# Hybrid RWKV-7 / S5 / expert trunk on one core: the experts' items worked in pairs, 512 moving columns a matmul, a pair's weights in two transfers

## Chip, cores, metric

One core of one Trainium2 chip. The metric is the device time of the one launch in microseconds. A result counts as faster or slower than before by the medians of runs of the two kernels on one chip.

## What is computed

The kernel runs a trunk of two residual layers on 256 tokens of width 1024, all in float32. Layer 0 is an RWKV-7 time mixer and a dense SwiGLU; layer 1 is an S5 state-space mixer and the expert SwiGLU, of which 2 of 8 experts take each token. The change is in the last of these:

```python
def moe_swiglu(x, router, w_gate, w_up, w_down):
    ...
    top_val, top_idx = lax.top_k(logits, TOP_K)
    gates = jax.nn.softmax(top_val, axis=-1)
    ...
    def block_ffn(args):
        tok, gate, e = args
        xb = xt[tok]
        h = jax.nn.silu(xb @ w_gate[e]) * (xb @ w_up[e])
        return (h @ w_down[e]) * gate[:, None].astype(x.dtype)
```

With D = 1024 and D_EXPERT = 3584, one expert's three matrices are 44 MB, the eight together 352 MB.

## The kernel before

The program is written engine by engine (SP issues DMAs, ACT, PE, DVE, POOL), with semaphores between them. The first 640 us are layer 0, the S5 mixer and its gated output; then come the router and the experts, which are all that the change touches, apart from one buffer's place.

**Blocks and items.** A block is 128 token slots of one expert. With these inputs each expert fills one block, so there are 8 blocks; the last ones go through a loop with a count from a register, with the same body. A block is worked in FM = 28 items. Item n stands for 128 of the 3584 hidden columns, and has 1.5 MB of weights: per partition 2048 floats of gate and up (part a) and 1024 floats of down (part b).

**Two-part numbers.** Every weight and activation is split in a high part, rounded to the matmul's float32r by a copy on ACT, and a low part, the rest by a subtraction on DVE. Each product is made of three matmuls: high by high, high by low, low by high.

**One item.**
- SP: `load_a` and `load_b` (L302, L305) bring parts a and b into one of 7 slots, EXA and EXB. Item n's loads wait until DVE has made the low parts of item n-7 (`m_alo`, `m_blo`): the split copies the weights into WHI and WLO, so the slot is free at once.
- ACT: `hi_a` (L554, two halves of 1024) and `hi_b` (L560) write WHI, of which there are 2; `gate` (L581) takes the silu of the gate half out of PSUM; `turned` (L585) rounds the turned hidden block.
- DVE: `lo_a` (L1650, two halves) and `lo_b` (L1656) write WLO; `product` (L1724) multiplies silu and up; `turned` (L1728) makes the low part of the hidden block.
- PE: `gate_up(n)` (L1180) is 24 matmuls with 256 moving columns (gate and up side by side, 8 k-chunks, 3 products each); `turn(n)` (L1189) transposes the 128x128 hidden block; `down(n)` (L1195) is 6 matmuls with 512 moving columns, added up in two PSUM banks over the 28 items.

**Order.** PE runs `gate_up(n)`, `turn(n-1)`, `down(n-2)` (L1246). ACT and DVE prepare item n+2 while PE works on n. The order on each engine is written out by hand in `first_step` and `steps`.

**Between blocks.** Ahead of a block's end PE gathers the next block's tokens by a one-hot matmul (`gather`, L1205, 16 x 2 matmuls in float32); ACT and DVE split them into XGH and XGL (`gathered`), on which the next `gate_up` waits. When the last `down` of a block is done, ACT and DVE scale and split its output (OH at L594, OL at L1738), and PE adds it to the stream by `scatter` (L1221) in two parts, with a DVE addition (L1744) after each.

Of the kernel before, what the change touches and what calls it, by code (L numbers as in the profile page):

```python
# [15 lines left out]
P = 128  # L16
# [14 lines left out]
NRING, NSLOT = 6, 7  # L31
# [5 lines left out]
FM = FE // P  # L37
WIDE, NARROW = 3 * D, 2 * D
# [39 lines left out]
def build(nc, xT, prm_d, con_d, wsq, wffn, wglu, wmoe, lora1_d, lora2_d, s5p_d, s5b_d, s5c_d, rout_d, out_d):  # L78
    with ExitStack() as ctx:
# [108 lines left out]
        SQG = at("SQG", [P, KC, T], F32, r(96))  # L188
# [7 lines left out]
        EXA = [at(f"EXA{n}", [P, NARROW], F32, o) for n, o in enumerate((r(0), r(8), r(16), r(24), r(32), 0, 8))]  # L196
        EXB = [at(f"EXB{n}", [P, D], F32, o) for n, o in enumerate((r(40), r(44), r(48), r(52), r(56), 16, 20))]
# [45 lines left out]
        def expert_in(part, b, n):  # L243
            return S(f"m{part}_in{n % NSLOT}"), (b * (FM // NSLOT) + n // NSLOT + 1) * 16

        def after(b, n):
            return (b, n) if n < FM else (b + 1, n - FM)

# [21 lines left out]
        def _(sp):  # L270
# [31 lines left out]
            def load_a(b, n, ex):  # L302
                sp.dma_start(EXA[n % NSLOT][:, :], wmoe[ex * FM + n][:, 0:NARROW]).then_inc(expert_in("a", b, n)[0], 16)

            def load_b(b, n, ex):  # L305
                sp.dma_start(EXB[n % NSLOT][:, :], wmoe[ex * FM + n][:, NARROW:WIDE]).then_inc(expert_in("b", b, n)[0], 16)

            sp.wait_ge(S("yq_ps"), KC)
            for n in range(5):
                load_a(0, n, 0)  # L310
                load_b(0, n, 0)
            load_a(0, 5, 0)
            sp.wait_ge(S("glu_used"), 2)
            load_b(0, 5, 0)
            load_a(0, 6, 0)
            load_b(0, 6, 0)
            for n in range(NSLOT, FM):
                sp.wait_ge(S("m_alo"), 2 * (n - NSLOT + 1))
                load_a(0, n, 0)
                sp.wait_ge(S("m_blo"), n - NSLOT + 1)  # L320
                load_b(0, n, 0)

            def load_block(b, ex):
                for n in range(FM):
                    sp.wait_ge(S("m_alo"), b * (2 * FM) + 2 * (n - NSLOT + 1))
                    load_a(b, n, ex)
                    sp.wait_ge(S("m_blo"), b * FM + n - NSLOT + 1)
                    load_b(b, n, ex)

# [12 lines left out]
        def _(act):  # L342
# [211 lines left out]
            def hi_a(b, n, h):  # L554
                if h == 0:
                    act.wait_ge(*expert_in("a", b, n))
                cols = slice(h * D, (h + 1) * D)
                act.activation(WHI[:, n % 2, cols], EXA[n % NSLOT][:, cols], ACT.Copy).then_inc(S("m_ahi"), 1)  # L558

            def hi_b(b, n, down_done=True):  # L560
                act.wait_ge(*expert_in("b", b, n))
                if down_done:
                    act.wait_ge(S("m_used"), b * FM + max(n - 1, 0))
                act.activation(WHI[:, n % 2, NARROW:WIDE], EXB[n % NSLOT][:, :], ACT.Copy).then_inc(S("m_bhi"), 1)  # L564
# [16 lines left out]
            def gate(b, n):  # L581
                act.wait_ge(S("m_ps2"), b * FM + n + 1)
                act.activation(MSG[:, n % 2, :], PS[:, n % 2, 0:P], ACT.Silu).then_inc(S("m_silu"), 1)  # L583

            def turned(b, n):  # L585
                act.wait_ge(S("ht_ps"), b * FM + n + 1)
                act.activation(MHH[:, n % 2, :], PS[:, 4, 0:P], ACT.Copy).then_inc(S("m_hh"), 1)

            def first_step(b, before):
                gate(b, 0)  # L590
                hi_a(b, 2, 0)
                if before:
                    act.wait_ge(S("m_used"), b * FM)
                    act.activation(OH[:, :], flat(PS[:, 2:4, :]), ACT.Copy, scale=GSL[:, 0:1]).then_inc(S("o_hi"), 1)  # L594
                hi_a(b, 2, 1)
                hi_b(b, 0, before)

            def steps(b, first, last):
                for n in range(1, FM):
                    gate(b, n)  # L600
                    turned(b, n - 1)
                    if n == FM - 1 and not last:
                        gathered(b + 1)
                    if n == FM - 1:
                        turned(b, n)
                    if n + 2 < FM or not last:
                        hi_a(*after(b, n + 2), 0)
                        hi_a(*after(b, n + 2), 1)
                    hi_b(b, n, not (first and n == 1))
                    if n == 5:  # L610
                        act.wait_ge(S("selt_ps"), b + 1)
                        act.activation(SELT[:, :], PS[:, 7, 0:T], ACT.Copy).then_inc(S("selt"), 1)

            gathered(0)
            first_step(0, False)
            steps(0, True, False)
            for b in range(1, NEXP - 2):
                first_step(b, True)
                steps(b, False, False)
            act.wait_ge(S("meta"), 1)  # L620
            last_block = act.value_load(META[0:1, 0:1], min_val=NEXP - 1, max_val=NEXP + 2)
            with act.Fori(NEXP - 2, last_block) as b:
                first_step(b, True)
                steps(b, False, False)
            first_step(last_block, True)
            steps(last_block, False, True)
            act.wait_ge(S("m_used"), (last_block + 1) * FM)
# [7 lines left out]
        def _(pe):  # L635
# [544 lines left out]
            def gate_up(b, n):  # L1180
                pe.wait_ge(S("m_alo"), b * (2 * FM) + 2 * n + 2)
                for k in range(KC):
                    cols = slice(k * T, (k + 1) * T)
                    for m, (x, w) in enumerate(((XGH, WHI), (XGH, WLO), (XGL, WHI))):
                        mm = pe.matmul(PS[:, n % 2, 0:T], x[:, k, :], w[:, n % 2, cols], start=k == 0 and m == 0,  # L1185
                                       stop=k == KC - 1 and m == 2)
                mm.then_inc(S("m_ps2"), 1)

            def turn(b, n, first=False):  # L1189
                pe.wait_ge(S("m_mul"), b * FM + n + 1)  # L1190
                if not first:
                    pe.wait_ge(S("m_hl"), b * FM + n)
                pe.transpose(PS[:, 4, 0:P], MHF[:, n % 2, :], ident).then_inc(S("ht_ps"), 1)  # L1193

            def down(b, n):  # L1195
                pe.wait_ge(S("m_blo"), b * FM + n + 1)
                pe.wait_ge(S("m_hl"), b * FM + n + 1)
                for c in range(2):
                    cols = slice(NARROW + c * 512, NARROW + (c + 1) * 512)
                    for m, (x, w) in enumerate(((MHH, WHI), (MHH, WLO), (MHL, WHI))):  # L1200
                        mm = pe.matmul(PS[:, 2 + c, :], x[:, n % 2, :], w[:, n % 2, cols], start=n == 0 and m == 0,  # L1201
                                       stop=n % FM == FM - 1 and m == 2, skip_group_check=True)
                mm.then_inc(S("m_used"), 1)
# [703 lines left out]
```

## Time and profile before

| | us |
|---|---|
| runs (3): median, lowest to highest | 1746.8, 1746.27 to 1753.04 |
| profiled execution, own time | 1744.34 |
| its span | 1742.5 |
| PE busy, share of the span | 1645.1, 94% |
| DVE busy | 1291.5, 74% |
| ACT busy | 975.0, 56% |
| bytes read, mean rate | 418.19 MB, 241 GB/s |

The 1.84 us between the span and the execution's own time lie outside what the profile covers. Busy shares are means over stages with different limits, so they say little of the experts' stage alone, which starts at about 650 us; that stage has to be read from the chain of waits and from the timelines of the engines inside one block. A busy time on PE counts a matmul as longer than it holds the engine, since matmuls overlap: what a matmul costs there is the distance from one start to the next.

### The profile page before, as it was taken

What the parts mean: (1) busy time and instruction counts of PE and PEld (TensorE: products, weight loads), DVE (VectorE), ACT (ScalarE), POOL (GpSimd) and SP (SyncE); (2) the same over time, 40 slices, a digit from 0 to 9 for tenths busy, and PEclk for the clock granted to TensorE, in tenths of its full rate; (3) what the DMA queues carried; (4) which work ended last, traced back from release to release, by engine and by line L of the source; (5) the groups of instructions that cost most, each with busy time, mean ns of one, the idle gap of its engine ahead of it and who ended that gap; (6) DMA issues with size and microseconds to landing.
All of it is one profiled execution on the core that took longest, in us unless ns stands there. A gap on an engine that the chain in (4) does not pass through costs nothing.

```text
span 1742.5 us, 35420 instructions
## 1 busy us (share of the span) xinstructions
PE 1645.1 (94%) x14954; PEld 1526.3 (88%) x14954; DVE 1291.5 (74%) x1878; ACT 975.0 (56%) x1476; POOL 83.9 (5%) x69
## 2 busy tenths in 40 slices
PE   6999799899998887999999999999999999999996
PEld 5788787899998767999999999999999999999995
DVE  6355433796866435888988988988988988988985
ACT  1332211577431123776776776776776776776774
POOL 0004300200003500000000000000000000000000
PEclk8999998999996996999999999999999999999998
DMA  7230001554524231998998998998998998998980
GB/s 308 73 121 2 4 4 29 190 191 150 181 86 195 97 159 62 356 355 307 352 361 307 349 363 304 352 362 306 353 357 302 353 363 309 347 361 308 350 324 25
DMA packets 76252, 421.53 MB, mean 242 GB/s; under 512 B 8624, under 2 KB 8880, under 8 KB 41280
## 3 DMA queue, kind: packets, MB, share of 16 engines
q1 hardware_dynamic: 75744, 418.18, 64.8%
q8 instruction: 119, 1.95, 0.4%
q0 software_dynamic: 352, 1.10, 0.2%
q14 instruction: 37, 0.30, 0.1%
HBM read 418.19 MB, written 1.05 MB: 241 GB/s over the span
## 4 chain that ended last, share of the span: by engine, by line
PE 86%; DVE 7%; ACT 2%; POOL 2%; issue 2%; DMA 0%; SPq 0%; DVEq 0%; POOLq 0%; ACTq 0%
PE PS L1185 33%; PE PS L1201 17%; PE PS L1023 11%; PE PS L657 5%; PE PS L1131 2%; DVE WLO L1653 2%; PE PS L1209 2%; PE PS L1008 2%; PE PS L1193 1%; PE PS L803 1%; DVE WLO L1658 1%; PE PS L639 1%; PE PS L820 1%; PE PS L1097 1%; PE PS L672 1%
## 5 line engine op out<-in xcount | busy, mean ns | idle before, releaser
L1653 DVE TENSOR_TENSOR WLO<-EXA,WHI 128x1024 fp32r<-128x1024 f32 x448 | 530.3, 1221 | 88.4 <-ACT WHI L558 87.8
L1185 PE MATMUL PS<-WHI,XGH 128*128 128x256 f32 x1792 | 510.0, 285 | 3.1 <-DVE XGL L1734 2.4
L1185 PE MATMUL PS<-WLO,XGH 128*128 128x256 f32 x1792 | 507.8, 283 | 0.0
L1185 PE MATMUL PS<-WHI,XGL 128*128 128x256 f32 x1792 | 507.7, 283 | 0.0
L558 ACT ACTIVATE WHI<-EXA 128x1024 fp32r<-128x1024 f32 x448 | 450.3, 1060 | 0.0
L1185 PEld LDWEIGHTS PS<-WHI,XGH 128*128 128x128 f32 x1792 | 340.8, 190 | 12.3 <-DVE XGL L1734 2.6
L1185 PEld LDWEIGHTS PS<-WLO,XGH 128*128 128x128 f32 x1792 | 340.6, 190 | 8.1
L1185 PEld LDWEIGHTS PS<-WHI,XGL 128*128 128x128 f32 x1792 | 340.7, 190 | 0.0
L1658 DVE TENSOR_TENSOR WLO<-EXB,WHI 128x1024 fp32r<-128x1024 f32 x224 | 273.0, 1219 | 2.4 <-ACT WHI L564 2.4
L564 ACT ACTIVATE WHI<-EXB 128x1024 fp32r<-128x1024 f32 x224 | 236.2, 1055 | 8.8 <-PE PS L1201 8.8
L583 ACT ACTIVATE MSG<-PS 128x128 f32<-128x128 f32 x224 | 62.1, 277 | 270.2 <-PE PS L1185 270.2
L1201 PE MATMUL PS<-WHI,MHH 128*128 128x512 f32 x448 | 195.3, 436 | 5.2 <-DVE WLO L1658 5.2
L1201 PE MATMUL PS<-WHI,MHL 128*128 128x512 f32 x448 | 176.9, 395 | 0.0
L1201 PE MATMUL PS<-WLO,MHH 128*128 128x512 f32 x448 | 175.4, 392 | 0.0
L1023 PE MATMUL PS<-FH,WHI 128*128 128x256 f32 x352 | 101.7, 289 | 6.1 <-DVE FL L1474 5.8
L1201 PEld LDWEIGHTS PS<-WHI,MHL 128*128 128x128 f32 x448 | 84.3, 188 | 19.8
L1023 PE MATMUL PS<-FL,WHI 128*128 128x256 f32 x352 | 100.5, 285 | 0.0
L1023 PE MATMUL PS<-FH,WLO 128*128 128x256 f32 x352 | 100.3, 285 | 0.0
L1201 PEld LDWEIGHTS PS<-WHI,MHH 128*128 128x128 f32 x448 | 84.3, 188 | 17.4 <-DVE WLO L1658 7.0
L1201 PEld LDWEIGHTS PS<-WLO,MHH 128*128 128x128 f32 x448 | 85.3, 190 | 10.3
L1726 DVE TENSOR_TENSOR MHF<-MSG,PS 128x128 f32<-128x128 f32 x224 | 62.8, 280 | 32.0 <-ACT MSG L583 32.0
L1023 PEld LDWEIGHTS PS<-FH,WHI 128*128 128x128 f32 x352 | 68.3, 194 | 6.9 <-issue 6.4
(370 smaller groups left out, 2398.4 us busy)
## 6 DMA issues: line engine op xcount, KB each, us to landing
EXA<-in_wmoe SPq DMA_DIRECT2D x224, 1024.0 KB, 7.8
EXB<-in_wmoe SPq DMA_DIRECT2D x224, 512.0 KB, 5.6
FRA<-in_wffn SPq DMA_DIRECT2D x22, 1024.0 KB, 5.8
RING<-in_wsq SPq DMA_DIRECT2D x16, 1024.0 KB, 4.9
FRB<-in_wffn SPq DMA_DIRECT2D x22, 512.0 KB, 3.7
GLUW<-in_wglu SPq DMA_DIRECT2D x8, 1024.0 KB, 12.2
LORA<-in_lora SPq DMA_DIRECT2D x1, 1536.0 KB, 22.1
LORA<-in_lora SPq DMA_DIRECT2D x1, 1152.0 KB, 18.9
```

Source lines behind the costliest of these rows:

```text
L558: act.activation(WHI[:, n % 2, cols], EXA[n % NSLOT][:, cols], ACT.Copy).then_inc(S("m_ahi"), 1)
L564: act.activation(WHI[:, n % 2, NARROW:WIDE], EXB[n % NSLOT][:, :], ACT.Copy).then_inc(S("m_bhi"), 1)
L583: act.activation(MSG[:, n % 2, :], PS[:, n % 2, 0:P], ACT.Silu).then_inc(S("m_silu"), 1)
L657: mm = pe.matmul(out, w[:, h * D + k * P:h * D + (k + 1) * P], x[:, k, :], start=k == 0, stop=k == KC - 1)
L1008: mm = pe.matmul(half(W_BANK[t - 12], h), w[:, h * D + k * P:h * D + (k + 1) * P], T1[:, k, :], start=k == 0, stop=k == KC - 1)
L1023: mm = pe.matmul(out, a, b, start=start and k == 0 and n == 0, stop=stop and k == k_count - 1 and n == 2, skip_group_check=True)
L1131: mm = pe.matmul(half(4 + t % 4, h), GLUW[:, t, h * D + k * P:h * D + (k + 1) * P], HN[:, k, :], start=first and h == 0 and k == chunks[0] ...
L1185: mm = pe.matmul(PS[:, n % 2, 0:T], x[:, k, :], w[:, n % 2, cols], start=k == 0 and m == 0, stop=k == KC - 1 and m == 2)
L1201: mm = pe.matmul(PS[:, 2 + c, :], x[:, n % 2, :], w[:, n % 2, cols], start=n == 0 and m == 0, stop=n % FM == FM - 1 and m == 2, skip_group ...
L1653: tt(WLO[:, n % 2, cols], EXA[n % NSLOT][:, cols], WHI[:, n % 2, cols].bitcast(F32), ALU.subtract)\
L1658: tt(WLO[:, n % 2, NARROW:WIDE], EXB[n % NSLOT][:, :], WHI[:, n % 2, NARROW:WIDE].bitcast(F32), ALU.subtract)\
L1726: tt(MHF[:, n % 2, :], MSG[:, n % 2, :], PS[:, n % 2, P:2 * P], ALU.mult).then_inc(S("m_mul"), 1)
```

## The change

Items are worked in pairs, 14 a block (NP). PE, ACT and DVE take a pair where they took an item:

- `gate_up(p)` is 24 matmuls with 512 moving columns, the two items' columns side by side (two runs of 256); one PSUM bank holds a pair. The transposes of the pair before stand in its middle, after 12 matmuls. `down(p)` is 12 matmuls of 512, as two `down` before.
- The high parts lie in WH (4 items). The low part is written over the loaded weights (LOA and LOB have the addresses of EXA and EXB), so WLO is gone and its room holds more of WH.
- A slot is now free only when PE is done with it: the load of part a waits for `m_ps2` (the `gate_up` of the slot's last user), that of part b for `m_used` (its `down`).
- There are 4 slots of two items; PAIR_SLOT gives pair p's slot. Slot 3 is used by pairs 3 and 13 alone, so a slot comes back after 4 pairs for p = 0 to 6 and after 3 pairs for p = 7 to 12.
- A transfer brings two items: 2 MB for part a, 1 MB for part b.
- ACT and DVE take a part a in one instruction of 2048 elements instead of two of 1024, and the silu, product and turned steps of a pair in one of 256 instead of two of 128.
- The first high and low parts of block 0 are no longer interleaved with the norm before the router (`root(3)`, `norm(3)`); SQG, the squares of that norm, lies elsewhere.

```diff
-NRING, NSLOT = 6, 7
+NP = FM // 2
+PAIR_SLOT = (0, 1, 2, 3, 0, 1, 2, 0, 1, 2, 0, 1, 2, 3)
...
+        EXA = [at(f"EXA{n}", [P, 2, NARROW], F32, o) for n, o in enumerate((r(0), r(16), r(32), 0))]
+        EXB = [at(f"EXB{n}", [P, 2, D], F32, o) for n, o in enumerate((r(48), r(100), 16, r(64)))]
+        LOA = [at(f"LOA{n}", [P, 2, NARROW], F32R, o) for n, o in enumerate((r(0), r(16), r(32), 0))]
+        LOB = [at(f"LOB{n}", [P, 2, D], F32R, o) for n, o in enumerate((r(48), r(100), 16, r(64)))]
+        WH = at("WH", [P, 4, WIDE], F32R, 24)
...
+        def slot_before(p):
+            return max(x for x in range(p - NP, p) if PAIR_SLOT[x % NP] == PAIR_SLOT[p])
...
+            def load_a(b, p, ex):
+                two = wmoe[bass.ds(ex * FM + 2 * p, 2)].rearrange("e p c -> p e c")
+                sp.dma_start(EXA[PAIR_SLOT[p]][:, :, :], two[:, :, 0:NARROW]).then_inc(expert_in("a", b, 2 * p)[0], 16)
...
+            def load_block(b, ex, first=False):
+                for p in range(NP + 1):
+                    if p < NP:
+                        if not first or slot_before(p) >= 0:
+                            sp.wait_ge(S("m_ps2"), b * NP + slot_before(p) + 1)
+                        elif p == 3:
+                            sp.wait_ge(S("glu_used"), 2)
+                        load_a(b, p, ex)
+                    if p > 0:
+                        if not first or slot_before(p - 1) >= 0:
+                            sp.wait_ge(S("m_used"), b * NP + slot_before(p - 1) + 1)
+                        elif p == 4:
+                            sp.wait_ge(S("xt_ps"), 2)
+                        load_b(b, p - 1, ex)
...
-            hi_a(0, 0, 0)
             root(3)
-            hi_a(0, 0, 1)
-            hi_a(0, 1, 0)
-            hi_a(0, 1, 1)
+            hi_a(0, 0)
+            hi_a(0, 1)
...
+            def step(b, p, first, last):
+                fresh = first and p == 0
+                gate(b, p)
+                if p == NP - 1 and not last:
+                    gathered(b + 1)
+                if p + 2 < NP or not last:
+                    hi_a(*after(b, p + 2)[:1], 2 * after(b, p + 2)[1])
+                if p == 0 and not first:
                     act.wait_ge(S("m_used"), b * NP)
                     act.activation(OH[:, :], flat(PS[:, 2:4, :]), ACT.Copy, scale=GSL[:, 0:1]).then_inc(S("o_hi"), 1)
+                if p + 2 < NP or not last:
+                    hi_a(after(b, p + 2)[0], 2 * after(b, p + 2)[1] + 1)
+                turned(b, p)
+                if p + 1 < NP or not last:
+                    if not fresh:
+                        act.wait_ge(S("m_used"), b * NP + p)
+                    for e in range(2):
+                        hi_b(after(b, p + 1)[0], 2 * after(b, p + 1)[1] + e)
...
+            def gate_up(b, p, turn_of=None):
+                pe.wait_ge(S("m_alo"), b * FM + 2 * p + 2)
                 for k in range(KC):
+                    if k == KC // 2 and turn_of:
+                        turn(*turn_of)
                     cols = slice(k * T, (k + 1) * T)
+                    hi, lo = WH[:, 2 * (p % 2):2 * (p % 2) + 2, cols], LOA[PAIR_SLOT[p]][:, :, cols]
+                    for m, (x, w) in enumerate(((XGH, hi), (XGH, lo), (XGL, hi))):
+                        mm = pe.matmul(PS[:, p % 2, :], x[:, k, :], w, start=k == 0 and m == 0, stop=k == KC - 1 and m == 2)
...
+            def block(b, first, last):
                 pe.wait_ge(S("xg_lo"), b + 1)
+                for p in range(NP):
+                    if p > 0:
+                        gate_up(b, p, (b, p - 1))
+                        if p == 1 and not first:
+                            scatter(b, 0)
+                        down(b, p - 1)
+                        if p == 1 and not first:
+                            scatter(b, 1)
+                    elif first:
+                        gate_up(b, 0)
+                    else:
+                        gate_up(b, 0, (b, -1))
+                        down(b, -1)
...
```

DVE's step follows the same order as ACT's: product, `lo_a` of item 2p+4, `lo_a` of item 2p+5, `turned`, `lo_b` of the two items of pair p+1; with `gathered` after the product in the last step, OL between the two `lo_a` in step 0, and the two additions (L1744) around the first `lo_a` in step 1.

**SP, the end of a block.** The built order of the transfer queue before, three slots on either side of block 0's end (all transfers wait for DVE's low parts; EXA is part a, EXB part b, the digit is the slot):

```order
L303 DMA EXA4_152<-in_wmoe 128x2048 [waits m_alo]
L306 DMA EXB4_159<-in_wmoe 128x1024 [waits m_blo]
L303 DMA EXA5_153<-in_wmoe 128x2048 [waits m_alo]
L306 DMA EXB5_160<-in_wmoe 128x1024 [waits m_blo]
L303 DMA EXA6_154<-in_wmoe 128x2048 [waits m_alo]
L306 DMA EXB6_161<-in_wmoe 128x1024 [waits m_blo]
```

and of the change, from pair 11 of block 0 to pair 1 of block 1:

```order
L314 DMA EXA1_149<-in_wmoe 128x2x2048 [waits m_ps2]
L318 DMA EXB0_152<-in_wmoe 128x2x1024 [waits m_used]
L314 DMA EXA2_150<-in_wmoe 128x2x2048 [waits m_ps2]
L318 DMA EXB1_153<-in_wmoe 128x2x1024 [waits m_used]
L314 DMA EXA3_151<-in_wmoe 128x2x2048 [waits m_ps2]
L318 DMA EXB2_154<-in_wmoe 128x2x1024 [waits m_used]
L318 DMA EXB3_155<-in_wmoe 128x2x1024 [waits m_used]
L314 DMA EXA0_148<-in_wmoe 128x2x2048 [waits m_ps2]
L314 DMA EXA1_149<-in_wmoe 128x2x2048 [waits m_ps2]
```

Part a of pair 11 is the first row, of pair 12 the third, of pair 13 the fifth (slot 3); the part a of the next block's pair 0 stands behind both last parts b.

**DVE, the first items of block 1.** Before:

```order
L1726 TENSOR_TENSOR MHF<-MSG,PS 128x128
L1653 TENSOR_TENSOR WLO<-EXA_150,WHI 128x1024
L1738 SCALAR_TENSOR_TENSOR OL<-PS,GSL,OH 128x1024
L1653 TENSOR_TENSOR WLO<-EXA_150,WHI 128x1024
L1658 TENSOR_TENSOR WLO<-EXB_155,WHI 128x1024
L1726 TENSOR_TENSOR MHF<-MSG,PS 128x128
L1730 TENSOR_TENSOR MHL<-PS,MHH 128x128
L1653 TENSOR_TENSOR WLO<-EXA_151,WHI 128x1024
L1744 TENSOR_TENSOR HT<-HT,PS 128x1024
```

and now, over the first two pairs:

```order
L1725 TENSOR_TENSOR MHF<-MSG,PS 128x256
L1650 TENSOR_TENSOR LOA_158<-EXA_150,WH 128x2048
L1738 SCALAR_TENSOR_TENSOR OL<-PS,GSL,OH 128x1024
L1650 TENSOR_TENSOR LOA_158<-EXA_150,WH 128x2048
L1730 TENSOR_TENSOR MHL<-PS,MHH 128x256
L1656 TENSOR_TENSOR LOB_161<-EXB_153,WH 128x1024 x2
L1725 TENSOR_TENSOR MHF<-MSG,PS 128x256
L1744 TENSOR_TENSOR HT<-HT,PS 128x1024
L1650 TENSOR_TENSOR LOA_159<-EXA_151,WH 128x2048
L1744 TENSOR_TENSOR HT<-HT,PS 128x1024
```

The output's split and the two additions now fall into two pairs' time where they fell into three items' time.

## Rows read from the trace of the kernel before

**Rows 1.** The page: 40 slices (PE, granted clock, DMA, GB/s)
```profile
PE   6999799899998887999999999999999999999996
PEclk8999998999996996999999999999999999999998
DMA  7230001554524231998998998998998998998980
GB/s 308 73 121 2 4 4 29 190 191 150 181 86 195 97 159 62 356 355 307 352 361 307 349 363 304 352 362 306 353 357 302 353 363 309 347 361 308 350 324 25
```
**Rows 2.** Chain of waits inside a block (start, us, what)
```profile
1248.02 2.88 PE PS L1185 x24
1250.90 0.11 PE PS L1193
1251.01 1.39 PE PS L1201 x6
1252.39 2.88 PE PS L1185 x24
```
**Rows 3.** Chain of waits at a block's end: gathers, a piece of down, scatter, slots
```profile
795.85 0.92 PE PS L1201 x4
796.77 3.57 PE PS L1209 x32
...
809.41 1.06 ACT WHI L558
...
816.91 1.28 DVE OL L1738
...
838.97 0.22 PE PS L1215 x2
839.18 0.34 PE PS L1217 x4
...
927.09 3.57 PE PS L1209 x32
```
**Rows 4.** DVE and ACT inside a block (start, us, engine, line, names)
```profile
1252.36 2.36 DVE L1653 TENSOR_TENSOR WLO<-EXA,WHI 128x1024 fp32r<-128x1024 f32 x2 [0.48 <-ACT WHI L558]
1254.63 1.22 DVE L1658 TENSOR_TENSOR WLO<-EXB,WHI 128x1024 fp32r<-128x1024 f32 x1
1255.31 0.28 ACT L583 ACTIVATE MSG<-PS 128x128 f32<-128x128 f32 x1 [1.09 <-PE PS L1185]
```
**Rows 5.** Groups by line and form: instructions of the sizes the change uses
```profile
L1361 DVE TENSOR_TENSOR KK<-KK,PS 128x2048 f32<-128x2048 f32 x1 | 2.3, 2287 | 5.4 <-PE PS L711 5.4
L1592 DVE TENSOR_TENSOR FHF<-FSG,PS 128x256 f32<-128x256 f32 x22 | 9.2, 419 | 21.2 <-ACT FSG L527 21.2
L612 ACT ACTIVATE SELT<-PS 128x256 fp32r<-128x256 f32 x8 | 3.0, 380 | 0.0
L378 ACT ACTIVATE KSQ<-KK x1: 1902/1902/1902, 77.4 to 77.4; 128x2048 f32<-128x2048 f32 x1
```
**Rows 6.** Block 0's first items, the norm before it, and the last items
```profile
645.48 1.28 ACT L348 ACT_TABLE_LOAD   x1
647.23 1.75 DVE L1292 RECIPROCAL NT<-NT 128x256 f32<-128x256 f32 x1 [0.29 <-ACT NT L348]
678.81 4.61 PE PS L1185 x24
688.20 0.08 DVE OV L1709
...
691.50 0.16 DVE META L1722
692.49 2.67 PE PS L1201 x6
1717.51 0.13 PE PS L1193
1720.20 1.67 PE PS L1201 x6
```
**Rows 7.** Windows: time, busy of five engines, clock, DMA share, GB/s
```profile
600.00:625.00 25.00, 25.00 (x118) 22.00 (x117) 4.54 (x10) 4.74 (x11) 0.00 (x0) 1.00 1.00 413
718.00:796.00 78.00, 78.00 (x557) 73.47 (x556) 69.86 (x90) 58.37 (x90) 0.00 (x0) 1.00 0.97 357
840.00:925.00 85.00, 85.00 (x607) 80.11 (x607) 75.88 (x102) 63.43 (x97) 0.00 (x0) 1.00 0.97 359
```
**Rows 8.** Part a of one item alone (issued at 598.4), and of 718 to 925 us
```profile
DMA to landing us min/median/max: 5.2/5.2/5.2
DMA to landing us min/median/max: 5.5/8.0/9.5
```

More of the change, by code:

```diff
@@ L598, in steps, with gate @@
-            def steps(b, first, last):
[L599 to L612, printed above, removed]
+            def gate(b, p):
+                act.wait_ge(S("m_ps2"), b * NP + p + 1)
+                act.activation(MSG[:, :, :], PS[:, p % 2, :].rearrange("p (e t) -> p e t", e=2)[:, :, 0:P], ACT.Silu)\
+                   .then_inc(S("m_silu"), 1)
@@ L1187, in gate_up, with turn @@
                 mm.then_inc(S("m_ps2"), 1)
[L1189 to L1202, printed above, removed]
+            def turn(b, p):
+                pe.wait_ge(S("m_mul"), b * NP + p + 1)
+                for e in range(2):
+                    tr = pe.transpose(PS[:, 4, e * P:(e + 1) * P], MHF[:, e, :], ident)
+                tr.then_inc(S("ht_ps"), 1)
@@ new lines, in down @@
+            def down(b, p):
+                pe.wait_ge(S("m_blo"), b * FM + 2 * p + 2)
+                pe.wait_ge(S("m_hl"), b * NP + p + 1)
+                for e in range(2):
+                    for c in range(2):
+                        cols = slice(c * 512, (c + 1) * 512)
+                        hi, lo = WH[:, (2 * p + e) % 4, NARROW + c * 512:NARROW + (c + 1) * 512], LOB[PAIR_SLOT[p % NP]][:, e, cols]
+                        for m, (x, w) in enumerate(((MHH, hi), (MHH, lo), (MHL, hi))):
+                            mm = pe.matmul(PS[:, 2 + c, :], x[:, e, :], w, start=p == 0 and e == 0 and m == 0,
+                                           stop=p % NP == NP - 1 and e == 1 and m == 2, skip_group_check=True)
@@ new lines, in step @@
+            def step(b, p, first, last):
+                product(b, p)
+                if p == NP - 1 and not last:
+                    gathered(b + 1)
+                if p == 1 and not first:
+                    add(b, 0)
+                more_a, more_b = p + 2 < NP or not last, p + 1 < NP or not last
+                if more_a:
+                    lo_a(after(b, p + 2)[0], 2 * after(b, p + 2)[1])
+                if p == 0 and not first:
+                    out_low(b)
+                if p == 1 and not first:
+                    add(b, 1)
+                if more_a:
+                    lo_a(after(b, p + 2)[0], 2 * after(b, p + 2)[1] + 1)
+                turned(b, p)
+                if more_b:
+                    for e in range(2):
+                        lo_b(after(b, p + 1)[0], 2 * after(b, p + 1)[1] + e)
+                if p == 3:
+                    dve.wait_ge(S("selt"), b + 1)
+                    dve.tensor_copy(GSL[:, :], PS[:, 7, T:T + 1]).then_inc(S("gsl"), 1)
+                if p == 4 and not last:
+                    dve.wait_ge(S("gsl"), b + 1)
+                    if isinstance(b, int):
+                        one_hot(b + 1)
+                    else:
+                        one_hot(dve.value_load(META[0:1, bass.ds(b + 13, 1)], min_val=0, max_val=2 * NEXP - 1))
@@ L1779, in _ @@
+            def steps(b, first, last):
+                for p in range(NP):
+                    step(b, p, first, last)
+                    if p == 0 and first:
+                        blocks_in_order()
             gathered(0)
-            first_step(0, False)
-            blocks_in_order()
+            lo_b(0, 0)
+            lo_b(0, 1)
             steps(0, True, False)
             for b in range(1, NEXP - 2):
-                first_step(b, True)
                 steps(b, False, False)
```

194 lines of the change are left out of this document (56 added, 138 removed).

## The prediction

> **What bounds the kernel now.** I read the slices first: from the seventeenth on, which is the experts' stage, PE is at 9, the granted clock is at its upper level (2.4 GHz), and the DMA digits repeat 9, 9, 8 with 302 to 363 GB/s [rows 1]. PE and DMA both look full, so the chain of waits has to say which one ends last. Inside a block it is PE alone: 24 matmuls of 256 columns in 2.88 us, a transpose in 0.11, six matmuls of 512 in 1.39, and at once the next item [rows 2]. An item takes 1252.39 - 1248.02 = 4.37 us, a block's 28 take 122.4. DVE is close behind: 2.36 + 1.22 us of low parts an item besides two small steps, with 0.48 us of idle that ends on ACT [rows 4]. DMA moves 1.5 MB an item, 357 to 359 GB/s, at a busy share of 0.97 [rows 7]; but it is paced by PE through the slots, and the same queue moved 413 GB/s at 600 to 625 us, when seven items were queued at once.
>
> From one gather to the next a block takes 927.09 - 796.77 = 130.3 us [rows 3]. Its PE work is 122.4 + 3.57 (gather) + 0.22 + 0.34 (slots) + 16 scatter matmuls of 256 columns at 0.12 = 1.92, in all 128.5. So PE stands for 1.8 us a block, all of it at the block's start, where the chain leaves PE for ACT and DVE [rows 3].
>
> **The change, part by part.** g is the moment at which PE ends `gate_up` of a pair.
>
> 1. *Matmul width.* A matmul of 256 columns costs 2.88 / 24 = 0.120 us [rows 2], one of 512 costs 0.92 / 4 = 0.230 [rows 3]. A pair's gate and up were 48 of the first (5.76) and are now 24 of the second (5.52): 0.24 us less a pair, 8 x 14 = 112 pairs, **-26.9 us**. Bounds: 0 if a moving operand in two runs of 256 costs what two matmuls did (0.240), -26.9 if it runs as that of `down`; no row shows less for 512. I take the second, since the engine, type and width are those of `down`. The Trainium skill (TensorE: Matmul & The Clock Gate, Back-to-back issue gap) gives an isolated gap of N / 2.4 + 2.5 ns. By it two matmuls of 256 would cost only 2.5 ns more than one of 512, 0.06 us a pair, and this term would be -6.7 us. The rows speak against it: 0.120 and 0.230 are 13 and 17 ns above N / 2.4, so joining two saves 10 ns. `down` keeps its 12 matmuls a pair, the two transposes keep 0.11 each.
>
> 2. *DVE and ACT inside a block.* An instruction of 2048 elements takes 2.29 us on DVE and 1.90 on ACT, one of 256 takes 0.42 and 0.38 [rows 5]; 1024 cost 1.22 and 1.06 [rows 4, 3]. A pair: DVE 2 x 2.29 + 2 x 1.22 + 2 x 0.42 = 7.9 us, ACT 2 x 1.90 + 2 x 1.06 + 2 x 0.38 = 6.7, against PE's 5.52 + 2.77 (12 x 0.231) + 0.22 = 8.51. Neither binds by its sum. In order: ACT's silu to g + 0.4, high parts to g + 4.2; PE transposes at g + 2.8 + 2.8 = g + 5.6, ACT's turned to g + 6.1, `hi_b` to g + 8.2. DVE's product to g + 0.9, low parts to g + 6.9, turned to g + 7.3, where `down` wants it at g + 8.5; `lo_b` to g + 9.7, the next product to g + 10.1, and the next low part can't start before g + 8.5 + 2.3 = g + 10.8. So PE has 1.2 us to spare and DVE 0.7. **0 us**. If that cover goes, `down` is late by what the low parts are late.
>
> 3. *Block starts.* XGL is ready at g + 0.4 + 1.0 + 1.2 = g + 2.7, PE wants it after `down` at g + 2.8: hidden by a tenth. In step 0 the output's split waits for the last `down` (g + 2.8): OH to g + 3.9, DVE's OL to 5.8; `scatter` part 0 is due after the next `gate_up` at g + 8.5. Then comes `down` (2.8), and part 1 waits for DVE's addition. The order shows it behind turned, two `lo_b` and a product: DVE is there at about g + 11, the addition ends at 12.3 beside `down`'s g + 12.2. PE stands some 0.3 us where it stood 1.8. Seven starts by 1.5: **-10.5 us** (bounds: 0, if DVE's backlog is carried on as now, and -12.6, all of it).
>
> 4. *Block 0's start.* Before, 678.8 to 796.8 was 118.0 us for 112.8 of work (26 `gate_up` at 2.88, 25 `down` at 1.39, 25 transposes, the slots): 5.2 lost, to the clock at its lower level (24 matmuls in 4.61 instead of 2.88, six in 2.67 [rows 6]) and to DVE's table of blocks (688.2 to 691.7 [rows 6]). Now that table stands behind step 0. By the durations of part 2: the first `gate_up` ends at 686.0, the second at 691.8, DVE's turned at 693.1 (PE waits 1.3); table to 698.8, product to 699.2, where the transposes want it at 698.7 (0.5); low parts and turned to 704.0 against a third `gate_up` at 702.2 (1.8). With the clock's 1.7 that is 5.3, and the stalls may cost clock again. **+0.5 us**, give or take 3.
>
> 5. *The norm before.* DVE's reciprocal came at 647.23 because a high part stood ahead of the square root and its table load [rows 6]. Without it the load can start 1 us earlier: **-0.9 us**. The high and low parts that stood there fit where ACT and DVE wait for PE's transposes and gather.
>
> 6. *The end.* After the last `gate_up` PE had one `down`, a transpose at 1717.51, and the last `down` at 1720.20, held by `lo_b` [rows 6]. Now `lo_b` was made a step earlier, and only the turned step is waited for, about 1.2 us: **-1.8 us**.
>
> 7. *Transfers.* The price no row gives. Slots are free later (after PE, not after DVE), so there are 3 or 4 pairs of lookahead less the time PE takes. Where it is 3 (pairs 7 to 12), part a of pair p+3 is issued at g(p), and ACT wants it at g(p+1) + 0.3 = g + 8.8. If it lands at g + L, the chain is L + 1.9 + 2.3 + 2.3 + 0.4 to `down`(p+1), then 2.8 and 5.5 to g(p+3), which is due at 25.5: PE waits only if L is over 10.2 us. Bounds for L: one item's part a, alone, took 5.2 us [rows 8]; another 1 MB at 413 GB/s is 2.5 more, 7.7. In the steady stretch it took 8.0 in the middle [rows 8], queued behind its predecessor; 1 MB more at 357 GB/s is 2.9, 10.9. The queue should be shorter than that, since part b of 1 MB was issued 5.7 us before, so I take 8.5 to 9: no wait, with 0.5 us a block for those that scatter past 10.2, **+4 us**. By rate: a block's 44 MB in 126 us is 350 GB/s, but SP issues nothing from g(2) + 2.8 to g(4), since pair 7 waits for slot 0's second user. Less 2.8 us for issue and landing, 21 MB must move from g(4) to ACT's use of pair 13 at g(11): 59.9 - 2.8 = 57.1 us, 367 GB/s.
>
> Sum: -26.9 - 10.5 + 0.5 - 0.9 - 1.8 + 4 = -35.6 us. The profiled execution took 1744.3, so 1708.7; it lies 2.5 us below the runs' median of 1746.8, from which the sum gives 1711.2. I say **1710 us**.
>
> **Rivals.**
> - *The transfers' rate takes over.* If the queue, under load from ACT and DVE, can't pass 358 GB/s, the 21 MB take 58.6 + 2.8 = 61.4 us where 59.9 are there: 1.5 us a block instead of 0.5, **1718 us**; at 350 GB/s it is 2.9 a block, 1729. For it: share 0.97 at 357 to 359, and landing at 8.0 us. Against it: 413 in the same queue. The Trainium skill (HBM Reference, Specifications (TRN2)) gives 358 GB/s as the effective rate of one core, and says that a core alone goes well above it. The trace's 413 agrees with the second. Chance 0.18.
> - *512 columns in two runs bring less.* A pair's gate and up at 5.7 us or more: **1730 to 1737 us**. The skill's isolated gap would put it at 1730. For it: the moving operand is no longer one run. Against it: [rows 2, 3]. Chance 0.12.
> - *A late transfer holds ACT: slower than before.* ACT waits for part a ahead of turned, so a late part a holds `down`, and with it the release of the next slots. Over L = 10.2 each pair of 7 to 12 is longer by (L - 10.2) / 3, a block by 2 x (L - 10.2). All of the gain (35.6 + 4 = 39.6, 4.9 a block) is gone at L = 12.7. If a transfer of two items takes as long as two of one item in the steady stretch less one fixed part (5.2 - 2.5 = 2.7, so 16.0 - 2.7 = 13.3 us), a block is 6.2 longer: **1757 us**. For it: no transfer of 2 MB in this trace, the two items' rows lie 1.5 MB apart, and the slots are fewer. Against it: the 8.0 us already hold a queue of one item. Chance 0.07.
> - That the change doesn't do what it says is ruled out by the built order: 24 matmuls of 128x512 a pair, and transfers of 128x2x2048.
>
> **How the numbers follow.** Forecast 0.58 (1701 to 1716; block 0's start and the other starts may each be 3 to 6 us off), the rate 0.18 (to 1729), the columns 0.12 (to 1738), late transfers 0.07 (half of it above 1755), anything else 0.05. About 0.5% (8.7 us) is what a measurement of this kernel can tell from no change. Faster, under 1738: 0.58 + 0.18 + 0.11 = 0.87. Within 0.5%: 0.01 of the columns' case, 0.03 of the late transfers', 0.02 of the rest, 0.06. Slower, over 1755.5: the other 0.04 of the late transfers' and 0.03 of the rest, 0.07. For 8 in 10 the range takes the forecast's, the rate's, and the columns' in part: 1701 to 1732.
>
> **What would show it.** In the profile after: `gate_up`'s 24 matmuls in 5.5 us and a pair every 8.5 us in the chain (5.76 says the columns bring nothing); gather to gather 126 us; PE's idle time at a block's start under 0.5 us; DVE idle ahead of each first low part by about a microsecond, ended by ACT; part a from issue to landing under 10 us, DMA near 370 GB/s in a block's second half and a hole in the first. ACT's first high part released by a DMA in most pairs would make me wrong toward the slower side. PE released by the turned low part inside a block would say that part 2 was cut too fine.

## The result and the profile after

| | before | after |
|---|---|---|
| median of 4 runs, us | 1746.5 | 1699.9 |
| lowest to highest | 1743.1 to 1753.0 | 1698.8 to 1704.5 |
| ratio, 95% interval | | 0.9734 (0.970 to 0.977) |
| span of the profiled execution | 1742.5 | 1697.9 |

The change makes the kernel 46.6 us faster by these medians. 35.6 were forecast, as 1710 us, with a range from 1701: the sign and the mechanism were right, the size wasn't, and the time lies 1 us outside the range. Two repetitions of the pair of kernels (e1 and e9 below) gave 41.7 and 41.9 us, with the change at 1701.6 and 1702.0 us. So the last 5 us of the gain are not firm, and the 1 us outside the range could have fallen either way; what was wrong in the forecast has to be read from the stages.

The slices of the page, against [rows 1]:

```profile
PE   5999789899998996999999999999999999999996
PEclk8999998899997897999999999999999999999998
...
GB/s 309 81 110 16 5 4 27 151 190 170 160 152 199 3 273 1 223 367 410 273 374 417 276 374 411 281 375 411 273 385 410 272 384 402 279 385 401 273 389 27
```

PE is still full. The transfers are less even than they were: a block's three slices read some 275, 375 and 410 GB/s, where they read some 305, 350 and 360. The first is the hole in the issues, where pair 7 waits for its slot; the last is above anything the steady stretches before had.

The chain of waits inside a block (start, us, what), against [rows 2]:

```profile
1219.87 2.72 PE PS L1208 x12
1222.59 2.72 PE PS L1191 x12
1225.31 0.22 PE PS L1197 x2
1225.53 2.75 PE PS L1191 x12
1228.28 2.72 PE PS L1208 x12
```

A pair takes 1228.28 - 1219.87 = 8.41 us. Two items took 8.75, and 8.51 were forecast. Twelve matmuls of 512 columns take 2.72 us, 0.2267 each: `down`'s (L1208) too, which cost 0.230 to 0.231 before. Only the twelve behind the transposes take 0.03 more.

The block's period and its start in the chain of waits, against [rows 3]; L1216 is the gather, L1234 and L1235 are scatter:

```profile
1040.69 3.57 PE PS L1216 x32
...
1165.30 3.57 PE PS L1216 x32
...
1177.29 2.95 PE PS L1191 x12
...
1192.58 2.75 PE PS L1208 x12
1195.33 0.10 issue
1195.43 0.36 PE PS L1234
```

Gather to gather is 124.61 us (130.3 before). 14 x 8.41 + 3.57 + 1.92 + 0.56 is 123.8, so PE loses 0.8 us at a block's start, in three places for the most part: 0.23 in the first `gate_up` (2.95 for 2.72), 0.34 around scatter's second part, and 0.14 in the twelve matmuls behind the slots (2.86 for 2.72 at 1214.04). It was 1.8.

The groups by line, against [rows 4, 5]:

```profile
L1650 DVE TENSOR_TENSOR LOA<-EXA,WH 128x2048 fp32r<-128x2048 f32 x224 | 504.5, 2288 | 87.0 <-ACT WH L563 87.0
L563 ACT ACTIVATE WH<-EXA 128x2048 fp32r<-128x2048 f32 x224 | 416.8, 1910 | 4.3 <-DMA EXA<-in_wmoe 3.9
```

The durations are those taken (2.29 and 1.90). DVE's idle ahead of the first low part of a pair is 87 us over 112 pairs, 0.8 each, and ends on ACT. ACT was held by a transfer 3.9 us in all, and PE never.

Block 0's start in the chain of waits, against [rows 6]; L1708 is the first of the table's instructions on DVE:

```profile
679.89 5.75 PE PS L1191 x24
...
692.71 2.27 DVE LOB L1656 x2
694.98 0.08 DVE OV L1708
...
698.43 0.32 DVE MHF L1725
698.75 4.40 DVE LOA L1650 x2
703.15 0.34 DVE MHL L1730
703.50 0.14 issue
703.63 3.00 PE PS L1208 x12
```

As walked: the table (from 694.98, L1708 on) between the low parts and the product, and `down` of pair 1 at 703.6, held by both.

**Where the 44.6 us of the two profiled executions lie**, from one marker of the chain to the next:

| stage | before | after | difference |
|---|---|---|---|
| start to the S5 output's matmuls | 598.35 | 601.42 | +3.07 |
| to the router's first matmul | 53.98 | 53.04 | -0.94 |
| to block 0's first `gate_up` | 26.48 | 25.43 | -1.05 |
| to the gather of block 1 | 117.96 | 111.61 | -6.35 |
| six blocks, gather to gather | 781.75 | 747.63 | -34.12 |
| last gather to the end | 163.98 | 158.77 | -5.21 |

The first row is code that the change doesn't touch. The later profiles put it anywhere from 593.7 to 604.1 us, so a single execution's span carries some 5 us either way that is nobody's doing, and I compare stages where less than that matters. The third row is chance too: it is block 0's gather, whose 32 matmuls took 6.27 us before and 5.22 after, at a granted clock of 0.56 (670 to 676 us) and 0.72 (672.3 to 677.5). In the later profiles of kernels with the change it took 5.17 to 6.76 us.

### The profile page after: what moved, and what is told of

It is laid out like the page before. It is cut to its first block, busy times and chain, and to the rows that moved or that the text cites. A ratio compares the mean times of both kernels' runs of the same rounds, so it can differ in the third digit from the quotient of the medians.

```text
span 1697.9 us, 28219 instructions
## 1 busy us (share of the span) xinstructions
PE 1607.5 (95%) x12266; PEld 1378.8 (81%) x12266; DVE 1257.5 (74%) x1430; ACT 942.0 (55%) x1028; POOL 83.9 (5%) x69
## 3 DMA queue, kind: packets, MB, share of 16 engines
HBM read 418.19 MB, written 1.05 MB: 247 GB/s over the span
## 4 chain that ended last, share of the span: by engine, by line
PE 91%; DVE 4%; POOL 2%; issue 1%; ACT 1%; DMA 0%; SPq 0%; POOLq 0%; DVEq 0%
PE PS L1191 36%; PE PS L1208 18%; PE PS L1026 11%; PE PS L660 5%; PE PS L1134 2%; PE PS L1011 2%; PE PS L1216 2%; PE PS L1197 1%; PE PS L642 1%; PE PS L806 1%; PE PS L823 1%; PE PS L1100 1%; PE PS L675 1%; PE PS L1234 1%; POOL SPS L1836 1%
## 5 line engine op out<-in xcount | busy, mean ns | idle before, releaser
L1650 DVE TENSOR_TENSOR LOA<-EXA,WH 128x2048 fp32r<-128x2048 f32 x224 | 504.5, 2288 | 87.0 <-ACT WH L563 87.0
L563 ACT ACTIVATE WH<-EXA 128x2048 fp32r<-128x2048 f32 x224 | 416.8, 1910 | 4.3 <-DMA EXA<-in_wmoe 3.9
L1191 PE MATMUL PS<-WH,XGH 128*128 128x512 f32 x896 | 360.8, 403 | 2.4 <-DVE XGL L1734 2.4
L1191 PE MATMUL PS<-WH,XGL 128*128 128x512 f32 x896 | 350.7, 391 | 0.0
L1191 PE MATMUL PS<-LOA,XGH 128*128 128x512 f32 x896 | 350.1, 391 | 0.0
L1656 DVE TENSOR_TENSOR LOB<-EXB,WH 128x1024 fp32r<-128x1024 f32 x224 | 264.2, 1221 | 8.5 <-ACT WH L567 8.5
L567 ACT ACTIVATE WH<-EXB 128x1024 fp32r<-128x1024 f32 x224 | 224.1, 1052 | 0.0
L1191 PEld LDWEIGHTS PS<-WH,XGL 128*128 128x128 f32 x896 | 168.2, 188 | 35.6
L1208 PE MATMUL PS<-WH,MHH 128*128 128x512 f32 x448 | 174.7, 390 | 4.2 <-DVE MHL L1730 4.2
L1208 PE MATMUL PS<-LOB,MHH 128*128 128x512 f32 x448 | 174.5, 389 | 0.0
L1208 PE MATMUL PS<-WH,MHL 128*128 128x512 f32 x448 | 174.4, 389 | 0.0
L1208 PEld LDWEIGHTS PS<-WH,MHH 128*128 128x128 f32 x448 | 84.1, 188 | 22.3 <-issue 5.2
L1208 PEld LDWEIGHTS PS<-WH,MHL 128*128 128x128 f32 x448 | 84.1, 188 | 17.5
L1208 PEld LDWEIGHTS PS<-LOB,MHH 128*128 128x128 f32 x448 | 84.2, 188 | 17.1
```

The costliest lines, as they stand in the source:

```text
L563: act.activation(WH[:, n % 4, 0:NARROW], EXA[PAIR_SLOT[n // 2]][:, n % 2, :], ACT.Copy).then_inc(S("m_ahi"), 1)
L567: act.activation(WH[:, n % 4, NARROW:WIDE], EXB[PAIR_SLOT[n // 2]][:, n % 2, :], ACT.Copy).then_inc(S("m_bhi"), 1)
L1191: mm = pe.matmul(PS[:, p % 2, :], x[:, k, :], w, start=k == 0 and m == 0, stop=k == KC - 1 and m == 2)
L1208: mm = pe.matmul(PS[:, 2 + c, :], x[:, e, :], w, start=p == 0 and e == 0 and m == 0, stop=p % NP == NP - 1 and e == 1 and m == 2, skip_gro ...
L1650: tt(LOA[slot][:, n % 2, :], EXA[slot][:, n % 2, :], WH[:, n % 4, 0:NARROW].bitcast(F32), ALU.subtract)\
L1656: tt(LOB[slot][:, n % 2, :], EXB[slot][:, n % 2, :], WH[:, n % 4, NARROW:WIDE].bitcast(F32), ALU.subtract)\
```

## Experiments

Theory: PE alone ends last inside a block; the gain is what 512 columns save a matmul, and the forecast took too high a price for a matmul of 512. Rivals: the gain comes from working in pairs whatever the width; the transfers' size or the larger instructions on ACT and DVE carry part of it; the transfers limit it.

**e1. The change once more.**

> The changed kernel itself, once more. Its 1699.9 us should come back within 0.3%. What varies from one profiled execution to the next is to be read from it: the experts' stage (gather to gather) at 124.60 us within 0.1 whatever the execution, and the start of the S5 output's matmuls (598.35 us before, 601.42 after, in code the change doesn't touch) anywhere within about 3 us if that shift was chance, at 601.4 again if the change made it.

Measured: 1701.6 us (ratio to before 0.9759, 0.9727 to 0.9791; the unchanged kernel measured 1743.3 here). Gather to gather was 124.60 us, and the S5 output's matmuls began at 597.75. A second repetition, e9, gave 1702.0 us (0.9751, 0.9725 to 0.9776), 124.60 and 593.65. The 3.07 us were chance; the block's period repeats to 0.02 us. Block 0's start doesn't repeat as well: its first 24 matmuls took 7.32 us in e1, at a granted clock of 0.77, and 5.75 in the first profile and in e9, at 1.00.

**e2. The width alone.**

```diff
                     for m, (x, w) in enumerate(((XGH, hi), (XGH, lo), (XGL, hi))):
-                        mm = pe.matmul(PS[:, p % 2, :], x[:, k, :], w, ...)
+                        for e in range(2):
+                            mm = pe.matmul(PS[:, p % 2, e * T:(e + 1) * T], x[:, k, :], w[:, e, :], ...)
```

> Pairs, buffers and transfers kept, but each matmul of 512 moving columns in gate_up made as two of 256 (the weights loaded twice). If the gain lies in the matmuls' width, at 0.120 us for 256 columns and 0.2267 for 512: 24 x 0.0133 = 0.32 us more a pair, a pair at 8.73, gather to gather 129.1, 112 pairs 36 us, 1736 us. If it lies in working in pairs (fewer waits, instructions and PSUM turns) and not in the width: 1700 to 1705 us. By the Trainium skill's isolated gap (TensorE: Matmul & The Clock Gate, Back-to-back issue gap) two of 256 cost 2.5 ns more than one of 512: 1707 us.

Measured: 1726.3 us (0.9886, 0.9861 to 0.9911), 24.7 above e1, whose neighbour in the same job it was; gather to gather 128.33. The chain of waits:

```profile
1252.48 2.87 PE PS L1192 x24
1255.35 0.22 PE PS L1200 x2
1255.57 2.88 PE PS L1192 x24
1258.44 2.75 PE PS L1211 x12
1261.19 2.88 PE PS L1192 x24
```

A pair takes 8.71 us, 0.30 more than in the change, and a block 3.73 more: 30 us over 8 blocks. (14 x 0.30 is 4.2; the rest comes back at a block's start. The stage from gather 0 to the end grew by 29.8; the medians' 24.7 has the chance of the first stages in it.) The expectation had 36 us and a block of 129.1. So the width carries 0.30 of the 0.34 us that a pair gained. The pair costs 0.04 less than two items even at 256 columns, and the timeline shows where: matmul starts in `down`, behind 256-column matmuls (start, duration, engine, line),

```profile
1258.28 0.40 PE L1211 MATMUL PS<-WH,MHH 128*128 128x512 f32 x1
1258.51 0.40 PE L1211 MATMUL PS<-LOB,MHH 128*128 128x512 f32 x1
...
1259.67 0.39 PE L1211 MATMUL PS<-WH,MHH 128*128 128x512 f32 x1
1259.89 0.39 PE L1211 MATMUL PS<-LOB,MHH 128*128 128x512 f32 x1
...
1261.03 0.40 PE L1192 MATMUL PS<-WH,XGH 128*128 128x256 f32 x2
```

The first six stand (1259.67 - 1258.28) / 6 = 0.232 us apart, the other six (1261.03 - 1259.67) / 6 = 0.227. Twice six (the down of two items) are all dear ones; of twelve in a row half are. By the isolated gap of the Trainium skill (TensorE: Matmul & The Clock Gate, Back-to-back issue gap), which the page gives for a single matmul, the width would be worth an estimated 6.7 us, and e2 less 6.7 is 1719.6. The change in the same job measured 1701.6, 18 us below it, so that gap doesn't describe matmuls which each load their weights, as these do.

**e3. One item a transfer.**

```diff
-                sp.dma_start(EXA[PAIR_SLOT[p]][:, :, :], two[:, :, 0:NARROW])...
+                for e in range(2):
+                    sp.dma_start(EXA[PAIR_SLOT[p]][:, e, :], two[:, e, 0:NARROW])...
```

(part b likewise, the waits for 32 instead of 16)

> Each transfer of two items made as two of one item, issued one behind the other behind the same wait. If the transfers are hidden and their size doesn't matter: 1700 us, within 3. If the two-item transfers are what lets the queue reach 410 GB/s: landing goes up from 7.7 us in the second half of a block to over 10, DMA back to under 370 GB/s over a block's last part, and the time by up to 1.6 us a block, 1713 us.

Measured: 1697.6 us (0.9726, 0.9702 to 0.975), gather to gather 124.60. The transfers' size is worth nothing here: they are hidden either way. Nor does the queue need transfers of two items for its rate: in the same part of the same block it moved 383 GB/s (1101 to 1166 us) where e1 moved 383 (1095 to 1160; e3's block begins 6 us later). Part a of one item landed in 7.2 us in the middle.

**e4. The kernel before with the transpose inside gate_up.**

```diff
                 for k in range(KC):
+                    if k == KC // 2 and turn_of:
+                        turn(*turn_of)
...
-                    gate_up(b, n)
-                    turn(b, n - 1)
+                    gate_up(b, n, (b, n - 1))
                     down(b, n - 2)
```

> The kernel before, with the transpose of the item before moved from behind gate_up into its middle, for the items from 3 on. Nothing is removed, so the time should stay at 1746 us, within 4. If a matmul of 512 columns in down took 0.230 us because it stands behind a transpose, down's six now take 0.2267 each (1.36 us), and the 256-column matmuls behind the transpose become a few ns longer. If the 0.230 belongs to down itself (its two banks, its six in a row), they stay at 0.230 and the pair's 0.2267 has another cause.

Measured: 1743.0 us (0.9989, 0.9976 to 1.0003). No transpose stands near `down` now (the timeline, start and duration):

```profile
1253.11 0.40 PE L1203 MATMUL PS<-WHI,MHH 128*128 128x512 f32 x1
1253.34 0.40 PE L1203 MATMUL PS<-WLO,MHH 128*128 128x512 f32 x1
...
1254.27 0.39 PE L1203 MATMUL PS<-WHI,MHL 128*128 128x512 f32 x1
1254.50 0.28 PE L1187 MATMUL PS<-WHI,XGH 128*128 128x256 f32 x1
```

(1254.50 - 1253.11) / 6 = 0.232: still slow. A transpose right ahead isn't needed for it. Nor does the price belong to `down` itself, whose twelve cost 0.2267 each inside a pair of the change. With e2 what is left of the tried causes is a matmul's place behind shorter ones: a matmul of 512 costs 0.232 as one of the first six behind matmuls of 256, and 0.2267 later. The change shows it too: `down` behind the 256-column matmuls of scatter (1192.58 above) takes 2.75 us and not 2.72. Behind the two transposes of the change the first matmul takes 0.31 and the next six again 0.232 each. What in PE makes it so stays open.

**e5. Part a in halves on ACT and DVE.** The edit puts back two instructions of 1024 for each of 2048 in `hi_a` and `lo_a`.

> Part a on ACT and DVE in two instructions of 1024 elements an item again, all else as in the change. DVE's pair grows by some 0.13 us and ACT's by 0.2, and DVE has 0.9 us of idle a pair that ends on ACT. If PE alone ends last: gather to gather 124.6 us, 1700 us within 3. If the larger instructions are part of the gain: up to 0.13 x 112 = 15 us more, 1715 us.

Measured: 1696.5 us (0.9718, 0.969 to 0.9746), gather to gather 124.27, 0.33 less than the change. The larger instructions are no part of the gain; they cost a little. DVE can begin on the first half a microsecond earlier, and at the block's start scatter's second part now finds its addition done: the pieces `1195.33 0.10 issue` and `1195.43 0.36` of the change are gone. The chain of waits at the same place:

```profile
1191.87 2.75 PE PS L1210 x12
1194.62 0.11 PE PS L1236
1194.73 0.12 PE PS L1237
```

**e6. The load of part a 2.7 us later, for pairs 7 to 12.**

```diff
+                        if 7 <= p <= 12:
+                            sp.wait_ge(S("m_used"), b * NP + slot_before(p))
-                        if not first or slot_before(p) >= 0:
+                        elif not first or slot_before(p) >= 0:
```

> Parts a of pairs 7 to 12 are issued behind the down that follows the slot's gate_up, 2.7 us later than now. Landing then is at g + 2.7 + 7.7 = g + 10.4. By the prediction's chain, with what the trace of the change measured (L + 6.8 to down, 2.7 and 5.7 to the third gate_up's end, due at 25.2), PE waits over L = 10.0: 0.13 us a pair, 0.8 us a block, gather to gather 125.4 us, 1706 us. If a late part a costs nothing before PE's own wait for it (m_alo, due at g + 19.5, which would let L go to 13): 124.6 and 1700.

Measured: 1723.5 us (0.9876, 0.9841 to 0.9912), gather to gather 127.4 to 128.1. The chain of waits now goes through the transfer:

```profile
1105.01 7.81 DMA EXA<-in_wmoe
1112.82 0.02 issue
1112.85 1.93 ACT WH L565
1114.77 0.02 issue
1114.80 4.49 DVE LOA L1652 x2
...
1119.77 3.02 PE PS L1210 x12
1122.78 0.02 issue
1122.80 7.62 DMA EXA<-in_wmoe
```

That a late transfer would decide here was right: 2.7 us more than the change are enough. The price wasn't, 3.0 us a block and not 0.8, and 1723.5 us and not 1706: the release is now a `down`, so the circle closes over two pairs (1122.80 - 1105.01 = 17.8 us for 16.8, three times a block) and not over three, and the waiting `down` takes 3.02 instead of 2.72. In the change itself part a is issued 2.7 us earlier than here, so its slack is less than that.

**e7. A pair later.**

```diff
-                            sp.wait_ge(S("m_ps2"), b * NP + slot_before(p) + 1)
+                            sp.wait_ge(S("m_ps2"), b * NP + slot_before(p) + (2 if 7 <= p <= 12 else 1))
```

> Parts a of pairs 7 to 12 wait for the gate_up one pair later, so the lookahead is two pairs there. By the same chain g(p+3) = g(p+1) + 7.7 + 15.2 = 22.9 us over two pairs where 16.8 are due: 6.1 us more for every second pair, three times a block, 18.3 us a block: gather to gather 142.9 us, 1846 us. If the transfers are hidden with a whole pair to spare: 124.6 and 1700. If PE waits for the low part alone (L up to 13, here 16.1): 3.1 us three times, 134 us and 1775 us.

Measured: 1904.5 us in one run, gather to gather 150.1 to 152.3, 26 us a block more instead of 18.3. Its chain of waits has three such pieces a block:

```profile
1199.79 7.85 DMA EXA<-in_wmoe
...
1214.58 4.41 PE PS L1208 x12
...
1224.72 7.73 DMA EXA<-in_wmoe
```

The circle goes the forecast's way, over two pairs, but it takes 24.9 us (and 27.2 the time before) and not 22.9. PE's timeline at the same place, and a row of the windows (time, busy of five engines, clock, DMA share, GB/s):

```profile
1214.58 0.76 PE L1208 MATMUL PS<-WH,MHH 128*128 128x512 f32 x1 [6.41 <-DVE MHL L1730]
1214.00:1216.00 2.00, 1.42 (x4) 1.17 (x5) 2.00 (x4) 0.19 (x1) 0.00 (x0) 0.50 0.99 414
```

The transfer, the high parts and the low parts take 15 us in the chain, but PE works on other pairs for more than half of it: it stands for 6.4 us here, for 7.7 at the block's first such wait and for 6.3 at the third. Behind that the granted clock reads 0.50, the lower level of 1.2 GHz, and the twelve matmuls of `down` take 4.4 to 5.5 us instead of 2.72, up to twice as long. That the clock would charge for the wait a second time was left out. (The wait and the clock are from a single execution.)

**e8. The table of blocks spread.** Its 19 instructions on DVE stand in threes behind steps 5 to 11 of block 0.

> DVE's table of blocks (19 small instructions, 3.5 us) no longer stands behind step 0 of block 0, but three instructions each behind steps 5 to 11, where DVE idles 0.9 us a pair. By the walk, down of pair 1 then starts at 701.2 in the change's own times instead of 703.6: 2.4 us less, and none given back later, from gather 0 to gather 1 119.5 us instead of 121.9, 1697.5 us. If the start is held by the low parts and the clock and not by the table: no difference between gather 0 and gather 1.

Measured: 1696.6 us (0.9716, 0.9693 to 0.974). In the chain of waits `down` of pair 1 (from 701.06) now follows the `gate_up` ahead of it at once:

```profile
679.41 5.76 PE PS L1191 x24
...
692.38 2.99 PE PS L1208 x12
695.37 2.72 PE PS L1191 x12
698.09 0.22 PE PS L1197 x2
698.31 2.75 PE PS L1191 x12
701.06 2.72 PE PS L1208 x12
```

From the first `gate_up` to the gather of block 1 it is 788.61 - 679.41 = 109.20 us, against 111.61: 2.41 less. The two executions are alike in the clock there, since the first 24 matmuls take 5.76 and 5.75 us.

**e10 and e11. Both together, and the gathered tokens in halves.** e11's edit makes XGH and XGL in two instructions of 512 elements, one for each PSUM bank; `gate_up` waits for the second before its fifth k-chunk.

> The table of blocks spread (2.4 us less in block 0, by e8) and part a in halves of 1024 (0.33 us a block less, by e5, since DVE's first half is ready before ACT has made the second, and the second part of scatter then finds its addition done). If the two add: gather to gather 124.27 us, the experts' stage 2.4 + 7 x 0.33 = 4.7 us shorter than in the change. If they hide one another: only one of the two differences shows.

> As e10, with the gathered tokens' high and low parts made in two halves, so that the next block's first gate_up starts on the first. Its first twelve matmuls took 2.95 us where 2.72 are due: if that is the wait for XGL, gather to gather falls by 0.23 us to 124.04, the time by 1.6. If the 0.23 is what matmuls cost behind down there, it stays at 124.27.

> The changed kernel beside the two below, on their chip. Gather to gather 124.60 us again, and the time 1697 to 1703 us with what comes before the experts anywhere within 3 us.

| | median, us | ratio to before, 95% | gather to gather, us |
|---|---|---|---|
| the change (e9) | 1702.0 | 0.9751 (0.9725 to 0.9776) | 124.60 |
| e10 | 1691.6 | 0.9709 (0.9689 to 0.9729) | 124.27 |
| e11 | 1687.5 | 0.9680 (0.9660 to 0.9699) | 124.03 |

Both parts of e10 add up: from the first `gate_up` to the gather it is 785.36 - 676.86 = 108.50 us, 3.1 less than the change. In e11 the first twelve matmuls of a block's first `gate_up` take 2.72 again, and the 0.23 us a block are gone. By the period of a block e11 is the fastest version that I have, with PE work of 123.8 us in 124.03; the medians of e10 and e11 alone, 4 us apart with 1.6 expected, have overlapping intervals.

## Why the prediction was right or wrong

Term by term, the profiled executions' own stages against the sum. What was measured adds up to -47.6, of which the chance of the first stage takes 3.1 back:

| part | forecast | measured | from |
|---|---|---|---|
| 1 and 2, inside the pairs | -26.9 | -37.6 | (8.746 - 8.41) x 112 |
| 3, block starts | -10.5 | -6.9 | (5.69 - 14 x 0.336) x 7 |
| 4, block 0 | +0.5 | -0.5 | 4.7 lost instead of 5.2 |
| 5, the norm | -0.9 | -0.94 | second stage of the table |
| 6, the end | -1.8 | -1.5 + 0.85 | 1.32 lost instead of 2.83, and a lower clock behind it |
| 7, transfers | +4 | 0 | PE waits for none |
| not forecast: the clock at block 0's gather | | -1.05 | third stage, chance |

**The step that failed is part 1's price.** It took 0.230 us for a matmul of 512 from `down`, "since the engine, type and width are those of `down`", and called it the lower bound because "no row shows less for 512". All of `down`'s rows stood behind 256-column matmuls, six at a time, and e2 and e4 show that just those are dearer: 0.232, against 0.2267 for the rest. The rows did hold a hint. A matmul of 256 stood 13.3 ns above N / 2.4, one of 512 stood 17 above it; the part read this as a cost of width and not of place. With 13.3 ns for both, a pair is 24 x (0.240 - 0.2267) = 0.32 us less for `gate_up`. Of that 0.03 goes to the six behind the transposes, and `down`, which the part left at its price, falls from 2.78 to 2.72 a pair: 0.34 measured, where 0.24 were forecast. So about half of the missing 10.7 us lie in `gate_up` and half in `down`. A bound from a group of one place in the program is no bound.

**Part 7's 4 us were not there.** For pairs 7 to 12 of six blocks (800 to 1540 us) L had a median of 7.8 us, against 8.5 to 9 taken: 27 of the 36 landed in 7.6 to 8.0, the rest in 8.2 to 9.1, and none past 10.2, for which the allowance stood. So the two-item transfer costs little more than the lower bound said, 7.7. The reason to go above it, landing at 8.0 for one item, was a queue that always held another item, as the part itself said. Without that allowance, and with the 10.7 us that part 1 was short, the sum would have been -26.9 - 10.7 - 10.5 + 0.5 - 0.9 - 1.8 = -50.3.

**Part 3 claimed too much.** OL, the addition and XGL fell as walked, to some tenths: each of the waits called hidden "by a tenth" or "beside" `down` came out as a wait of 0.2 to 0.3 us, and the restart behind a stop wasn't in the walk (the first matmul of scatter's second part takes 0.36 us and the next ones 0.12). 0.8 us a block stayed, not 0.3.

**Part 5 held, 6 nearly, and 4 as a walk.** The low parts and the table held `down` of pair 1 until 703.6, at a distance of 23.7 from the start of the first `gate_up` (25.2 in the walk). The difference is the clock: the walk had 7.2 us for that `gate_up`, and this execution 5.75. Where it took 7.32, in e1, the distance was 25.3. So the -0.5 against the forecast +0.5 hangs on the clock of the execution: e9 took 111.6 us there as well, but e1 113.2, which is 1.1 lost more than in the kernel before. e8 then took away what the walk gave for the table, 2.41 us for 2.4. At the end, from the last `gate_up` to the end of the last `down`, PE lost 2.83 us beyond its work before and 1.32 after, 1.5 less where 1.8 were forecast. The first part of scatter behind it took 2.09 us instead of 1.24, as at the lower level (granted clock 0.50 at 1680 to 1684 us), which the part left out.

**The rivals.** The transfers' rate didn't take over: the queue moved 417 GB/s in one slice under full load from ACT, DVE and PE. So the busy share of 0.97 at 357 GB/s was not saturation. The Trainium skill's 358 GB/s (HBM Reference, Specifications (TRN2)) is no limit of one core alone, as the page itself says. The columns brought more, not less. The late transfer is real as a mechanism, and e6 finds it less than 2.7 us away; the forecast's L = 10.2 for it and the measured median of 7.8 are 2.4 apart. Its price past that point was too low: e6 cost 3.0 us a block for 0.8, since the circle closed over two pairs and not three, and e7 26 for 18.3, for the most part since the clock was left out.

## What to carry to other kernels

Take a matmul's price from rows that stand where the new ones will: behind the same neighbours and in runs of the same length, start to start. The rate of a queue that is paced by slots says nothing of its ceiling, whatever its busy share; look for a stretch where many transfers were queued at once. When two stretches of two profiles are compared, lay them at the same place of the same block first. A wait in the chain is not the time for which the engine stood: that is read from the engine's own timeline. When instructions merge, look at what their first half used to release: at a block's start two instructions of 1024 beat one of 2048.

## What I had not expected of the hardware

- A matmul of 512 columns (float32r, weights loaded before each) takes 0.232 us as one of the first six behind 256-column matmuls, and 0.2267 from the seventh on. Behind two transposes the first took 0.31, the next six 0.232.
- The busy share of the DMA engines read 0.97 at 357 GB/s and 0.98 at 383 (e1, 1095 to 1160 us), in stretches with the same work on ACT and DVE: it hardly moves with the rate.
- Where PE stood for 6.3 to 7.7 us in e7, it cost another 1.7 to 2.7 us, since the twelve matmuls behind it took 4.4 to 5.5 us instead of 2.72, at a granted clock of 0.50 to begin with. In e6, behind a wait of 0.68 us at a granted clock of 1.00, they took 3.02.
